# Experts' weights as runs of 8192 bytes: another layout of w13 and w2 in HBM

## The reference, cut to what matters

```
g_idx  = argmax over 4 groups of (h @ w_group + b_group)
top_i  = the 2 largest of the group's 8 experts, by h @ w_router + b_router
for each of the 32 experts e, for the tokens sent to it:
    a, b = split(x @ w13[e])          # w13: 32 x 1024 x 1024
    y    = (silu(a) * b) @ w2[e]      # w2:  32 x 512 x 1024
out[token] = sum over its two experts of gate * y
```

## Time and profile before

| what | us |
|---|---|
| median of 3 runs | 2355.97 (2354.79 to 2361.44) |
| span of the profiled execution | 2356.3 |
| route and experts, weight loads issued | 522.0 to 1153.0 |
| first and last y store issued | 591.0, 1182.6 |

### The profile page before, as it was taken

One profiled execution on the slowest core, in us unless ns is written; L12 is line 12 of the kernel. 1 busy time (PEld: TensorE's weight loads), 2 busy tenths in 40 slices (PEclk: granted clock), 3 DMA queues, 4 the chain that ended last, 5 costly groups with the idle time before them and its releaser, 6 DMA issues. The chain is left out here.

```text
span 2356.3 us, 43499 instructions
## 1 busy us (share of the span) xinstructions
PE 2145.3 (91%) x15936; PEld 1602.9 (68%) x15936; DVE 1237.3 (53%) x1539; ACT 823.3 (35%) x1198; POOL 564.1 (24%) x379
## 2 busy tenths in 40 slices
PE   5999988995787997878779989899999999999998
PEld 4788766783444554434458867688888888888887
DVE  7888356425676886757746458534332123212244
ACT  5122165113566885756622038512100001000023
POOL 1433211310000000000025632123323323233243
PEclk9999999996898998988869999999999999999999
DMA  7633042329999699999752300111111111111113
GB/s 276 245 126 118 28 161 66 134 90 409 410 360 333 242 380 353 355 356 354 293 194 90 95 26 1 34 47 45 45 53 45 47 51 45 54 45 52 47 56 123
DMA packets 104883, 370.12 MB, mean 157 GB/s; under 512 B 7948, under 2 KB 19052, under 8 KB 104428
## 3 DMA queue, kind: packets, MB, share of 16 engines
q1 hardware_dynamic: 86476, 326.68, 38.7%
q10 hardware_dynamic: 13008, 23.07, 2.6%
q0 software_dynamic: 5328, 19.40, 2.2%
HBM read 337.61 MB, written 31.51 MB: 157 GB/s over the span
## 5 line engine op out<-in xcount | busy, mean ns | idle before, releaser
L1673 PE MATMUL moe_hu<-x_res,moe_xt 128*32 128x256 f32 x5120 | 338.0, 407 | 63.6 <-DVE moe_xt L1592 24.1
L1570 DVE COPY x_res<-moew_raw 128x2048 f32 x243 | 270.4, 1135 | 171.4 <-DMA moew_raw<-in_w 106.0
L1673 PEld LDWEIGHTS moe_hu<-x_res,moe_xt 128*32 128x32 f32 x5120 | 162.5, 115 | 194.9 <-issue 58.7
L244 PE MATMUL ff_acc<-ff_yh,ff_w_hi 128*128 128x512 f32 x704 | 274.4, 390 | 0.0
L244 PE MATMUL ff_acc<-ff_yl,ff_w_hi 128*128 128x512 f32 x704 | 273.9, 389 | 0.0
L244 PE MATMUL ff_acc<-ff_yh,ff_w_lo 128*128 128x512 f32 x704 | 273.9, 389 | 0.0
L1570 ACT ACTIVATE x_res<-moew_raw 128x2048 f32 (+1 forms) x121 | 197.7, 1634 | 97.8 <-DMA moew_raw<-in_w 69.6
L212 POOL CAST ff_w_hi<-ff_w_raw 128x1024 fp32r<-128x1024 f32 (+1 forms) x82 | 81.9, 998 | 547.1 <-PE ff_acc L244 547.1
L244 PE MATMUL ff_acc<-xh,ff_w_hi 128*128 128x512 f32 x480 | 188.2, 392 | 3.3 <-DVE ff_w_lo L228 2.6
L214 POOL TENSOR_TENSOR ff_w_lo<-ff_w_raw,ff_w_hi 128x1024 fp32r<-128x1024 f32 (+1 forms) x82 | 188.6, 2300 | 6.6
L244 PE MATMUL ff_acc<-xl,ff_w_hi 128*128 128x512 f32 x480 | 187.3, 390 | 0.0
(11 more groups left out here) (426 smaller groups left out, 3734.4 us busy)
## 6 DMA issues: line engine op xcount, KB each, us to landing
moew_raw<-in_w SPq DMA_DIRECT2D x192, 1024.0 KB
ff_w_raw<-in_w_up SPq DMA_DIRECT2D x44, 512.0 KB, 3.5
mid_w_raw<-in_w_qkv SPq DMA_DIRECT2D x24, 512.0 KB
in_w_raw<-in_w_in SPq DMA_DIRECT2D x23, 512.0 KB, 3.6
xbc<-in_w_ada SPq DMA_DIRECT2D x20, 512.0 KB, 7.9
y_scratch<-acc_sq ACTq DMA_DIRECT2D x80, 128.0 KB
ff_w_raw<-in_w_down SPq DMA_DIRECT2D x16, 512.0 KB, 3.6
x_res<-in_w_ada SPq DMA_DIRECT2D x14, 512.0 KB, 4.1
```

The source lines that it names most:

```text
L244: m = pe.matmul(o, w[:, b, k * P:(k + 1) * P], x[:, k, h:h + HALF], start=(k == 0 and t == 0), stop=(k == kt - 1 and t == 2))
L1570: m = e.activation(to, src, ACT.Copy) if k == "act" else e.tensor_copy(to, src)
L1673: m = e.matmul(hu[u % 2][rows(j), 0:2 * FW].rearrange("p (a f) -> p a f", a=2), xt[:, t, rows(u)], w[:, :, FW * j:FW * (j + 1)], start=(t ...
```

## The change

The host writes w13 and w2 in another order: for each pair, partition p's two rows, 128a + p for a = 0 and 1, side by side. A load then brings one run of 8192 bytes to each partition. Number, size and order of the loads, the slots and every wait stay. The bytes in SBUF are the same.

```diff
-                        e.dma_start(self.raw[:, n, :].rearrange("p (a d) -> p a d", a=2), self.expert_pair(o, p)).then_inc(self.s_w[p], 16)
+                        e.dma_start(self.raw[:, n, :], self.expert_pair(o, p)).then_inc(self.s_w[p], 16)
...
     def expert_pair(self, x, p):
 
-        src, at = (self.ins["w13"], 2 * P * p) if p < KT // 2 else (self.ins["w2"], 2 * P * (p - KT // 2))
-        rows = src[x, at:at + 2 * P, :] if isinstance(x, int) else src[bass.ds(x, 1), at:at + 2 * P, :].rearrange("o r d -> (o r) d")
-        return rows.rearrange("(a p) d -> p a d", p=P)
+        src, n = (self.ins["w13"], p) if p < KT // 2 else (self.ins["w2"], p - KT // 2)
+        return src[x, n] if isinstance(x, int) else src[bass.ds(x, 1), n].rearrange("o p d -> (o p) d")
...
-                        e.dma_start(dst.rearrange("p (a d) -> p a d", a=2), self.expert_pair(source, p)).then_inc(s_w[p], 16)
+                        e.dma_start(dst, self.expert_pair(source, p)).then_inc(s_w[p], 16)
...
+def pairs(w):
+
+    E, K, N = w.shape
+    return np.ascontiguousarray(w.reshape(E, K // (2 * P), 2, P, N).transpose(0, 1, 3, 2, 4)).reshape(E, K // (2 * P), P, 2 * N)
...
-        "w13": np.ascontiguousarray(a["w13"][0]), "w2": np.ascontiguousarray(a["w2"][0]),
+        "w13": pairs(a["w13"][0]), "w2": pairs(a["w2"][0]),
```

## The result

Median 2367.74 us of 7 runs (2360.76 to 2376.13) against 2357.51 us of 7 runs of the kernel before: ratio 1.004, 95% interval 1.002 to 1.0059. The change makes the kernel 10 us slower. Forecast was slower by 25 us. The sign and the main mechanism held; the size did not. TensorE's granted clock is no part of the loss: it was 0.951 to 0.955 in the runs of the changed kernel and 0.944 to 0.949 in those of the kernel before.

A forecast was written before the change was run, and what follows sets the result against it. The weight stream was taken to bound two stretches, paced by four engines shared with y stores, and the units the middle. Terms -2 + 14 + 10 + 3 = +25 us on 2356.3 gave 2381 us; bounds 2349 to 2416.

The forecast's parts named there:

- (a): Weight loads in the two DMA-bound stretches: 8 KB packets cost less per byte, gain 0 to 7 us, taken as 2.
- (c): Expert stage: slower y stores hold up VectorE's y_out, costing 14 us in the first stretch, 10 from 790 to 1150 us.
- (d): Start of the expert stage: h_scratch stores land later and delay the gather, cost 0 to 7 us, taken as 3.
- much slower: Rival at the y stores: ScalarE blocks because its queue takes no fourth store; 2404 us, chance 0.14.
- Faster: Rival at the weight stream: loads take 2.91 instead of 3.17 us, fewer than four stores outstanding; 2343 us, chance 0.11.
- No change: Rival at the DMA engines: they share by bytes, or the ring's pauses pay everything back; 2357 us, chance 0.13.

The follow-up runs named there:

- e1: 8192-byte weight runs, each y store cut into four DMAs over all 16 engines, against the kernel before: 2280.57 us, ratio 0.9666.
- e2: 4096-byte weight runs as in the kernel before, each y store cut into four DMAs over all 16 engines: 2287.45 us, ratio 0.9695 to before.
- e10: The changed kernel, but y_out waits for the store three units back instead of four: 2401.3 us, ratio 1.0189 to the kernel before.
- e6: Kernel before with each y store issued as two DMAs of 512-byte pieces on the same four engines, 66 packets instead of 33: 2410.55 us, ratio 1.0224.
- e4: 8192-byte runs only for the routing stage's 17 loads, 4096-byte runs for the experts stage's 175: 2357.8 us, ratio 1.0001 to the kernel before.

## Why the prediction was right or wrong

The views led to the right cause. The y stores' 25.0% share, the counts of 19 to 19, and the turn of 191 ns gave a turn of 350 ns (335 measured over 20 us, 348 from packet to packet), stores that fall behind, waits for weights that vanish and a DMA share that drops in pauses. Each link has its row, and the experiments bear out the main ones: with wide stores the sign turns (e1 against e2), and fewer stores under way make the kernel slower by themselves (e10). e6 fits, with the two things in it that are not separated.

Of the 25 us forecast, 10 came. The steps that failed are (a), the size of the gain in bytes; (c), whose second part was twice too large; and (d), a cost at a place that is not in the path.

(a) Bytes, forecast -2 us. The step that failed is "8 KB being nearer to 4 than to 32". The bounds of the forecast, 0 to 0.05 us of 2.54, reach from 412 to 420 GB/s, and the 2 us that I took mean 414; measured are 422. The packets' own times show why. Most packets of 1, 2, 4, 8 and 32 KB took 46, 84, 159, 309 and 1213 ns, and a completion 9 ns: some 9 ns per packet and 37 ns per KB. So each doubling saves half of what the one before it saved, and more than half of what 32 KB can give comes with the first: 4 KB cost 159, 154.5 and 151.6 ns in rows of 4, 8 and 32 KB. Two numbers of the prediction had it already. 45 ns at 1 KB and 159 ns at 4 KB lie on a line that gives 311 ns at 8 KB, 7 less than two packets of 4 KB, and 136 x 8 x 7 ns are 8 us. The upper bound was too low too: the 1245 ns at 32 KB are a mean of 77 packets, of which 72 took 1213 to 1232 ns and five took 1418 to 1916. At 1213 ns the bound is 136 x 16 x 7.4 ns = 16 us.

In time the bytes are worth 7 to 11 us. e1 is 7 us faster than e2 in the medians. In the single traces it needs 173.5 us from the first to the 27th y store and e2 179.0, and from there to the 78th 325.9 and 331.8, which is 11.4 us less; but e1 also starts 5 us later (73.8 against 68.7 us from the first load to the first y store), and how much of the 11.4 is this delay paid back is not separated.

The rule of the Trainium skill that I weighed ("DMA: Bandwidth & Descriptors", "Why small descriptors are slow (HBM only)": 3 cycles per packet) gave 1.1% from 4 to 8 KB. The tables show 2.4% for that step and 4.8% from 2 to 4 KB, about twice the rule each time, in the rule's proportion of one to two.

(c) The stores' delay, forecast 14 + 10 = 24 us. What the narrow stores cost the new layout is its difference to before, +10, less what it gives with wide stores, -7: 17 us. The single traces split it. Between the same issues the changed kernel needs 204.1 and 380.9 us, and the kernel before 199.6 and 381.3. Wide stores save the new layout 30.6 and 55.0 us there, and the old one 20.6 and 49.5. So the narrow stores cost the new layout 10.0 us more in the first part, forecast 14, and 5.5 more in the second, forecast 10. This takes for granted that bytes and start are worth the same beside both kinds of stores. Why the second part cost half of the forecast is argued and not shown: the prediction itself allowed 0 there, because the ring is full when the part begins and the stores drain in each pause.

The path was in part another than (c) named. It had VectorE wait for the store four units back. VectorE waited 36.8 us there, 5.0 at the longest and not up to 11; the larger part, 103 us, was spent by ScalarE in issues that its full queue blocked.

(d) The start, forecast +3: 3.4 us later in the trace of after (72.4 us against 69.0 from the first load to the first y store), but in e4, which starts later still, the whole kernel is not slower, within 0.13%. A delay in front of a stretch that waits for another resource cost nothing here; I counted it as if it were in the path.

Together, in medians: (a) and (d), the layout where the stores don't matter, were forecast at +1 us and are -7; (c) was forecast at +24 and is +17. These are 8 and 7 of the missing 15 us. The two misses point the same way; that the sign held is owed to (c) being the large term.

Of the rivals, "much slower" named a thing that happens, ScalarE blocked because its queue is full at the fourth store, but not at the price of 23 us on top of the forecast. "Faster" failed because four stores were under way in many places. "No change" by another order of turns (the Trainium skill, same page, "Queues, rings and completion order": 9 to 17 descriptors before a switch) is contradicted by the single y packets that start 348 ns apart, one weight packet between them, and by the row that the prediction took for it: 19 to 19 in 6 us are five of each queue on an engine, fewer than nine. The 395 to 393 of different length rule out sharing by bytes.

Open is how much of e6's 51 us is ScalarE's second issue and how much the extra packets, and how the queue's depth is ruled. Not tried: more than four y buffers, and stores issued by another engine than ScalarE.

## What to carry to other kernels

Look in the queue tables for a DMA whose share stops at a fraction of the engines: here stores of 128 KB on four of 16 engines held a 192 MB weight stream at 357 instead of 412 GB/s (before and e2, 900 to 950 us). Making that store wide, by cutting it into four DMAs of 32 partitions to 32 rows, brought 3.0% alone (e2) and 3.3% together with the longer runs (e1, 2280.57 us, the fastest version here). Longer runs helped the stream that has them by 2.4% and took the turn of a y packet beside it from 191 to 335 ns, so first count the packets of what shares the engines and how many of them may be under way.

## What the runs showed of the hardware

- A DMA engine served two busy queues one packet in turn, whatever the length: 556 to 555 at 4 KB each, 395 to 393 at 8 and 4 KB, 19 to 19 at 32 and 1 KB; beside rows of 8 KB the 1 KB packets of one engine start 348 ns apart.
- Most packets of 1, 2, 4, 8 and 32 KB took 46, 84, 159, 309 and 1213 ns, and a completion 9 ns.
- A DMA issue on ScalarE's queue blocked the engine, for up to 7.59 us (8.94 in e6), when some hundred packets were waiting on one DMA engine (counted in two kernels, with 33 and 66 packets per store); the count at which it blocks is not fixed.
- With wide stores beside them, weights in rows of 2, 4 and 8 KB came with 393, 412 and 422 GB/s in all.
- A store of 128 partitions to a destination of 4 x 32 rows of 1 KB was moved by four engines (a share of 25.0%, 4 completions), and one of 32 partitions to 32 rows by all 16 (16 completions); it landed after 5.5 us.
